# Mask products behind the first mixer's scores, x read and normed first, expert items with two more tiles split ahead of the rows, and an end cut into halves and tiles

## The reference

```
for l in range(DEPTH):                       # first block, DEPTH = 2
    x = x + 0.5 * swiglu(rms_norm(x, ffn1_norm[l]), ffn1_w_in[l], ffn1_w_out[l])
    x = x + hybrid_mixer(rms_norm(x, mix_norm[l]), ...)
    x = x + 0.5 * swiglu(rms_norm(x, ffn2_norm[l]), ...)
```

## Time and profile before

| | us |
|---|---|
| median of 3 runs | 3257.64 (3256.85 to 3260.03) |
| the profiled execution | 3253.87 |
| its span in the trace | 3252.1 |
| PE busy | 3055.1 (94%) |
| DVE busy | 2228.5 (69%) |
| ACT busy | 1767.4 (54%) |
| HBM read | 680.10 MB, 210 GB/s over the span |

### The profile page before, as it was taken

The page is one execution under the profiler, slowest core; times in us unless marked ns, Lnnn a source line. Parts: engine busy times, 40 slices in busy tenths (PEclk is TensorE's granted clock), DMA queues, the critical chain, the costliest instruction groups (busy, mean ns, idle before and its releaser), DMA issues.

```text
span 3252.1 us, 51295 instructions
## 1 busy us (share of the span) xinstructions
PE 3055.1 (94%) x18945; PEld 2671.6 (82%) x18945; DVE 2228.5 (69%) x3150; ACT 1767.4 (54%) x2462; POOL 23.1 (1%) x46
## 2 busy tenths in 40 slices
PE   6999899899989999989999999889989999999996
PEld 5988788799878978888979988787968888888885
DVE  4665665566656666557566676566568998888985
ACT  4345443444544446456444453355467787777874
POOL 0000000000000000000000000000000000000000
PEclk9998999999989999999999999999989999999998
DMA  6863364786425855364578665434459999999995
GB/s 199 270 188 104 104 190 143 256 266 187 150 72 175 252 156 162 104 166 122 162 226 270 190 189 158 137 102 134 117 213 328 363 341 337 340 330 357 342 337 205
DMA packets 662298, 686.63 MB, mean 211 GB/s; under 512 B 22132, under 2 KB 517636, under 8 KB 660804
## 3 DMA queue, kind: packets, MB, share of 16 engines
q1 hardware_dynamic: 658512, 665.22, 63.9%
q0 software_dynamic: 3264, 18.55, 1.6%
q10 hardware_dynamic: 308, 0.09, 0.0%
HBM read 680.10 MB, written 3.67 MB: 210 GB/s over the span
## 4 chain that ended last, share of the span: by engine, by line
PE 82%; DVE 9%; ACT 4%; issue 3%; DMA 1%; DVEq 1%; SPq 0%; ACTq 0%; POOL 0%
PE W L622 30%; PE ACC L622 18%; PE W L705 15%; PE W L706 7%; PE W L615 4%; PE ACC L615 4%; DVE wlo L1626 2%; ACT whi L1211 1%; PE ACC L1015 1%; DVE TT L1652 1%; DVE R L1645 1%; DVE HB L1648 1%; PE ACC L1024 1%; DVE wlo L2047 1%; PE W L1033 1%
## 5 line engine op out<-in xcount | busy, mean ns | idle before, releaser
L1626 DVE TENSOR_TENSOR wlo<-raw,whi 128x1024 fp32r<-128x1024 f32 (+3 forms) x684 | 769.1, 1144 | 487.6 <-ACT whi L1211 485.9
L705 PE MATMUL W<-HB,whi 128*128 128x512 f32 x2112 | 764.2, 404 | 25.7 <-DVE HB L1648 15.7
L1211 ACT ACTIVATE whi<-raw 128x1024 fp32r<-128x1024 f32 (+3 forms) x684 | 658.2, 984 | 66.4 <-DMA raw<-in_ffn_w_in 35.5
L2047 DVE TENSOR_TENSOR wlo<-raw,whi 128x1024 fp32r<-128x1024 f32 x528 | 616.6, 1222 | 85.7 <-ACT whi L1497 79.8
L706 PE MATMUL W<-HB,wlo 128*128 128x256 f32 x2112 | 597.6, 283 | 0.0
L1497 ACT ACTIVATE whi<-raw 128x1024 fp32r<-128x1024 f32 x528 | 544.4, 1059 | 87.0 <-PE W L622 41.1
L622 PE MATMUL W<-HB,whi 128*128 128x256 f32 x2640 | 499.8, 292 | 22.4 <-DVE HB L1648 16.4
L705 PEld LDWEIGHTS W<-HB,whi 128*128 128x128 f32 x2112 | 401.1, 190 | 134.5 <-issue 21.7
L622 PE MATMUL W<-whi,HB 128*128 128x512 f32 (+1 forms) x1664 | 480.6, 374 | 16.5 <-DVE wlo L2047 15.3
L622 PEld LDWEIGHTS W<-HB,whi 128*128 128x128 f32 x2640 | 422.8, 197 | 33.6 <-issue 20.7
L706 PEld LDWEIGHTS W<-HB,wlo 128*128 128x128 f32 x2112 | 404.5, 192 | 0.0
(11 more groups left out here) (385 smaller groups left out, 4023.9 us busy)
## 6 DMA issues: line engine op xcount, KB each, us to landing
raw<-in_moe_w_gate SPq DMA_DIRECT2D x183, 512.0 KB, 5.1
raw<-in_moe_w_up SPq DMA_DIRECT2D x180, 512.0 KB, 5.4
raw<-in_ffn_w_in SPq DMA_DIRECT2D x176, 512.0 KB, 4.1
raw<-in_moe_w_down SPq DMA_DIRECT2D x176, 512.0 KB, 5.4
raw<-in_w_in SPq DMA_DIRECT2D x105, 512.0 KB, 4.1
raw<-in_ffn_w_out SPq DMA_DIRECT2D x88, 512.0 KB, 3.5
scratch<-in_w_mod SPq DMA_DIRECT2D x54, 512.0 KB, 6.9
raw<-in_mix_w_in SPq DMA_DIRECT2D x48, 512.0 KB, 3.7
```

What stands on the lines that cost most here:

```text
L705: mm(o, wh[:, w], HB[:, k, :], start=k == 0, stop=False, skip_group_check=True)
L1211: A_(whi[:, g % SPLIT, 0:LONG[g]], raw[:, g % RAW, 0:LONG[g]], ACT.Copy).then_inc(weight_high, 1)
L1626: V.tensor_tensor(wlo[:, g % RAW, 0:LONG[g]], raw[:, g % RAW, 0:LONG[g]], whi[:, g % SPLIT, 0:LONG[g]].bitcast(F32), ALU.subtract).then_in ...
L2047: V.tensor_tensor(wlo[:, g % RAW, :], raw[:, g % RAW, :], whi[:, g % SPLIT, :].bitcast(F32), ALU.subtract).then_inc(weight_split, 1)
```

## The change

It has four parts.

1. **First mixer.** In `scores` the products of four heads stand back to back and the eight mask products behind them; the second product of a head no longer starts its bank anew. `ret_scores`, `ret_values` and `values` are reordered so that two heads on different halves of the rows or columns alternate. On PE, `sums(0)` moves behind `column(14)`, `rotated` behind `rows(17)`, `sums(1)` behind `column(19)`. `sums(1)` waits for `rot_taken` (the rotation has read ACC) instead of `rot_done`, and `ret_scores` waits for `rot_done`. On ACT the exponential leaves `take` and becomes `invert`, one step later for the first four heads; `soften(0)` and both `weigh` move one step later. On DVE `rotate_all` moves from step 17 to 18.
2. **Start.** SP reads x in two halves first, then 8 vectors, then weights. ACT reads the identity. POOL reads the other 28 vectors, the context and the tables. PE waits for the identity and x alone, ACT squares straight out of PSUM, DVE copies x. Only two units are split ahead of the norm instead of five. The remaining vectors are transposed behind the first `up` unit of the first feed-forward (`first_step(0)`), the context in four pieces behind the units of f = 2 to 5, each copied by ACT one step later. The first modulation reads come at unit 30 instead of 24 and wait for the context's copy; PE waits for the tables only behind this feed-forward.
3. **Expert items.** ACT and DVE split two units (`upto(AHEAD + 2)`, `AHEAD` = 5) before `split_rows`; before, ACT split none and DVE one.
4. **End.** The last rows are weighed, rounded and subtracted in halves; the eight scattered tiles go to eight places, so that no tile waits for a buffer; add, square, sum, scale and transpose run tile by tile, and the output leaves in four DMAs from SP. ACT waits for the unused weight reads later.

```diff
 def scores(i):
-    for b in range(4):
-        h = 4 * i + b
-        q, k = QK1[side(h), h // 2, :], QK1[side(h), 4 + h // 2, :]
-        f32(ACC4[:, b, 0:256], k[:, 0:128], q, True, False)
-        mm(ACC4[:, b, 0:128], identR[:, :], negR[:, :], start=False, stop=True, skip_group_check=True)
-        f32(ACC4[:, b, 256:384], k[:, 128:256], q[:, 128:256], True, False)
-        last = mm(ACC4[:, b, 256:384], identR[:, :], negR[:, :], start=False, stop=True,
-                  skip_group_check=True)
+    for b, q, k in heads:
+        f32(ACC4[:, b, 0:256], k[:, 0:128], q, True, False)
+    for b, q, k in heads:
+        f32(ACC4[:, b, 256:384], k[:, 128:256], q[:, 128:256], False, False)
+    for b in range(4):
+        for c in (0, 256):
+            last = mm(ACC4[:, b, c:c + 128], identR[:, :], negR[:, :], start=False, stop=True,
+                      skip_group_check=True)
...
 def sums(i):
     if i == 1:
-        pe.wait_ge(rot_done, l + 1)
+        pe.wait_ge(rot_taken, l + 1)
...
 column(13)
+column(14)
 sums(0)
-column(14)
 column(15)
 rows(16, 4, 256, 0)
+rows(17, 4, 256, 4)
 rotated()
-rows(17, 4, 256, 4)
 column(18)
+column(19)
 sums(1)
-column(19)
...
 # DVE, step n of mix1
-if n == 17:
+if n == 18:
     rotate_all()
...
 # PE, behind unit "up" f of the first feed-forward
+def first_step(f):
+    if f == 0:
+        pe.wait_ge(vectors_in, 16 * N_VECTORS)
+        for t, n in ((1, 94), (2, 96), (3, 106), (4, 72)):
+            last = nc.tensor.transpose(o[:, t * 128 - 128:t * 128 - 128 + n], rows[0:n, t, :], ident[0:n, 0:n])
+        last.then_inc(params_turned, 1)
+    if 2 <= f < 6:
+        pe.wait_ge(params_taken, 1)
+        if f > 2:
+            pe.wait_ge(c_copied, f - 2)
+        for k in (2 * f - 4, 2 * f - 3):
+            for a in range(2):
...
 # POOL
+for dst, src in vectors[FIRST_V:]:
+    pool.dma_start(dst, src).then_inc(vectors_in, 16)
...
 # DVE, before the first feed-forward
+dve.wait_ge(gains_turned, 1)
 for l in range(2):
-    norm(X, ..., told=l == 1, ahead=start["ffn1", l] + AHEAD)
+    norm(X, ..., told=True, ahead=start["ffn1", l] + (AHEAD if l else 2))
...
 # ACT and DVE, item
-upto(SPLIT)                # DVE only
+upto(AHEAD + 2)
 split_rows()
...
 # DVE, end
-weigh_rows()
-split_rows()
-add_tiles(0).then_inc(dve_to_pe, 1)
-add_tiles(1)
+for c in range(2):
+    V.tensor_scalar(Y[:, c * 512:(c + 1) * 512], YP[:, c * 512:(c + 1) * 512], now[:, 4:5], None, ALU.mult
+                    ).then_inc(rows_weighed, 1)
...
+for d in range(KT):
+    dve.wait_ge(scattered, d // 4 + 1)
...
```

More of the change, by code:

```diff
@@ L488, in program @@
         assert at == 72
-        N_CONST, N_VECTORS = len(CONSTS) + 1, 3 + len(vectors)
-        HALF_V = len(vectors) // 2
+        FIRST_V = 8
+        N_CONST, N_VECTORS = len(CONSTS) + 1, 1 + len(vectors) - FIRST_V
         @block.sync
@@ L566, in _ @@
                     load(MOE + FFU + n, units[n], i)
+            for half in range(2):
+                for a in range(2):
+                    sp.wait_ge(out_copied, 2 * half + a + 1)
+                    cols2 = slice(half * 512, half * 512 + 512)
+                    sp.dma_start(out[0, a * 128:(a + 1) * 128, cols2], S[:, a * 1024 + half * 512:a * 1024 + half * 512 + 512]
+                                 ).then_inc(stored, 16)
+            sp.wait_ge(stored, 64)
         @block.gpsimd
@@ L602, in _ @@
                     pool.dma_start(S[:, 2816:5376], kept[l]).then_inc(kept_in, 16)
-            for a in range(2):
-                pool.wait_ge(act_to_pool, heard.next("act_to_pool"))
-                pool.dma_start(out[0, a * 128:(a + 1) * 128, :], S[:, a * 1024:(a + 1) * 1024]).then_inc(stored, 16)
-            pool.wait_ge(stored, 32)
         @block.tensor
@@ L708, in ffn @@
                     last.then_inc(weight_used, 1)
+                    if name == ("ffn1", 0) and kind == "up":
+                        first_step(f)
                     if name in FILTERS:
@@ L786, in ret_scores @@
                     pe.wait_ge(cum_taken, 2 * l + 2)
-                    for h in range(4):
-                        q, k = QKR[side(h), h // 2, :], QKR[side(h), 2 + h // 2, :]
+                    pe.wait_ge(rot_done, l + 1)
+                    heads = [(h, QKR[side(h), h // 2, :], QKR[side(h), 2 + h // 2, :]) for h in range(4)]
+                    for h, q, k in heads:
                         f32(ACC4[:, h, 0:256], k[:, 0:128], q)
+                    for h, q, k in heads:
                         last = f32(ACC4[:, h, 256:384], k[:, 128:256], q[:, 128:256])
@@ L1269, in ffn, with first_step @@
                 upto(p + N + AHEAD - 1)
+            def first_step(f):
+                if f == 2:
+                    act.wait_ge(params_taken, 1)
+                    for i in range(2):
+                        A_(CS[:, :, i], PV[:, 3, 90 + 8 * i:98 + 8 * i], ACT.Silu)
+                if 3 <= f < 7:
+                    act.wait_ge(c_turned, f - 2)
+                    A_(C[:, 2 * f - 6:2 * f - 4, :], W[:, 3, :].rearrange("p (k t) -> p k t", k=2), ACT.Copy).then_inc(c_copied, 1)
             def mix1(l):
@@ L1527, in item @@
                 upto(FFU + AHEAD)
-            for dst, src in vectors[HALF_V:]:
-                act.dma_start(dst, src).then_inc(vectors_in, 16)
-            act.wait_ge(pe_to_act, heard.next("pe_to_act"))
+            act.dma_start(ident[:, :], A["k_ident"]).then_inc(ident_in, 16)
             for b in range(4):
-                A_(X[:, 2 * b:2 * b + 2, :], ACC[:, 2 * b:2 * b + 2, :], ACT.Copy)
-            act.wait_ge(dve_to_act, heard.next("dve_to_act"))
-            for i in range(2):
-                A_(CS[:, :, i], PV[:, 3, 90 + 8 * i:98 + 8 * i], ACT.Silu)
-            act.wait_ge(pe_to_act, heard.next("pe_to_act"))
-            for b in range(4):
-                A_(C[:, 2 * b:2 * b + 2, :], W[:, b, :].rearrange("p (k t) -> p k t", k=2), ACT.Copy)
-            tell("act_to_pe")
-            tell("act_done")
-            act.wait_ge(act_done, heard.next("act_done"))
+                act.wait_ge(x_turned, b + 1)
+                A_(TT[:, 2 * b:2 * b + 2, :], ACC[:, 2 * b:2 * b + 2, :], ACT.Square).then_inc(x_squared, 1)
             for l in range(2):
-                norm(X, dst=Hhi, after="tiles" if l else "one", ahead=start["ffn1", l] + AHEAD)
+                norm(X, dst=Hhi, after="tiles" if l else "squared", ahead=start["ffn1", l] + (AHEAD if l else 2))
                 if l == 1:
```

190 lines of the change are left out of this document (123 added, 67 removed).

## The result

| | us |
|---|---|
| before, median of 4 runs | 3257.24 (3253.96 to 3260.03) |
| after, median of 4 runs | 3148.10 (3146.69 to 3150.52) |
| after / before | 0.9666, 95% interval 0.9649 to 0.9683 |
| the profiled executions, before and after | 3253.87 and 3147.45 |
| their spans | 3252.1 and 3145.6 |

The change takes 109 us off the median and 106.5 off the span. I had forecast 3173 and a range of 3154 to 3200. The direction, the places and nearly every mechanism were right.

A forecast was written before the change was run, and what follows sets the result against it. PE was taken to bound the kernel, busy 94% of the span, with four places idle or slow. Start 13, mixers 45, pairs 1.5, items 12.5 and end 12 make 84 us less: 3173 us, range 3154 to 3200.

The forecast's parts named there:

- Scores: First mixer: the two scores fall from 7.02 and 9.29 us to 2.9 each, giving back 10.5 us a layer.
- masks at 0.3 each: Mixer scores, bound from the other side: each mask keeps 0.3 us, making 4.1 us a call.
- Clock: Mixer: low-clock excesses of 2.3 (four columns), 1.4 (column 13) and 1.7 (`sums(1)`), 5.4 us a layer, go if PE stays dense.
- Gaps: Mixer: PE's gaps fall from 13.1 us a layer to 0.3, 0.3, 4.2 (before `sums(1)`) and 1.5.
- DVE is the late one: Mixer behind `logits(0)`: DVE needs 2.9 us a step, just PE's 2.88 a unit, plus five long operations.
- Layer 1: Second layer's mixer: the same stretch taken as 78.74 us, to become 22.7 us shorter.
- Pairs: Alternated pairs in `ret_values` and `values`: 0.25 us in each four heads, 1.5 us in all, nothing as lower bound.
- Start: Program start: first product at 22.2, 20.4 us earlier; 4.6 (transposes) and 2.5 (catching up, waits) given back; net 13, between 4 and 18.
- rival 4: Start: POOL's 29 vector DMAs land one behind the other, PE stands from 31 to 158, 3300 us; chance 0.02.
- Items: Expert items: PE's waits for split weights, 15.3 us, shrink to 0.3 at unit 7 per item; gain 12.5, between 0 and 15.3.
- End: Program end: work by halves and tiles, sums at 5.6 us, output finished at 3240; gain 12 us, between 8 and 15.
- Rivals 1 to 3: Mixer gaps stay 13.1 a layer, 3187 (0.14); masks dear and clock low, 3197 (0.09); items gain nothing, 3185 (0.11).

The follow-up runs named there:

- the new order alone: The kernel before with only the order of products and masks in the scores as after; median 3229.12 us.
- head by head: The kernel after with each head's two 64-row products followed by its two masks, 8 changes of rows a call; median 3163.85 us.

## Why the prediction was right or wrong

**What bounds the kernel** was read rightly: the four places with idle or slow PE are where all but some 4 us of the gain lie. The miss is in the sizes. The steps that failed are, largest first, the mixer's gaps (6.3 a layer for a measured 3.55) with layer 1's window (78.74 for 82.18), what the start gives back (7.1 for 3.4), and the durations at the end (12 us less for 16). One by one:

**Scores.** Right in the mechanism and near in size: 2.45 for my 2.9. The bound of masks at 0.3 each falls; they cost 0.11. The price per change was put at 0.28 at most; at clock 1.00 a head of before takes 1.55 (271.50 to 273.05 in its trace), of after 0.61, which is 0.27 for each of 14 changes, and head by head it is 0.40, over that bound.

**Clock.** Right for scores and columns: it is 1.00 through them, and the new order alone brings it back. Wrong for `sums(1)`. Its 1.7 us of excess were to go, with 0.6 given back, and they stayed: behind its wait it takes 5.22 for the 5.27 of before, in after as follows.

```profile
298.98:304.20 5.22, 5.22 (x25) 4.76 (x26) 5.22 (x9) 0.52 (x1) 0.00 (x0) 0.68 0.01 2
```

That the whole of PE's time still fits, 15.1 less in layer 0 (65.50 to 50.41) for my 15.9 less 0.6, is luck: the two calls took 0.9 less than I had, and that covers the 1.1 of `sums(1)`.

**Gaps.** This is the first mis-sized term. The step "DVE is the late one" gave 6.3 us of gaps a layer (0.3, 0.3, 4.2 and 1.5); there are 3.55. The wait before `sums(1)` is 3.17, the one before the retention's scores does not exist, and ACT's evacuation keeps up with the columns. The walk charged DVE 2.9 us for a split and four taps; back to back they take 2.72 in after (292.63 to 295.35). So DVE has read the rotation 43.3 us after the first scores, for my 44.6, and `logits(1)` ends at 50.9, for my 52.5 and before PE is there at 51.5. What the walk did get right is where the one large wait stands, and on whom; the second one, of 1.5, did not come. The terms of the stretch, 49.6, 6.3 and 0.6, also make 56.5 and not the 56 that I wrote.

**Layer 1.** "Layer 1 has the same stretch in 78.74" was false. I ended the window at 947 by the length of layer 0 and did not look for the retention's scores, which start at 950.44. The stretch is 82.18 because the clock was 0.81 in it. The error is 3.4 us, and the row itself had a hint: 374 matmuls where layer 0 has 381.

**Pairs.** 1.5 predicted, 0.16 a layer measured in the one place that shows them alone. What else is in the 4.3 of that row are the two waits of 0.77 and the 1.5 that comes and goes, once in each layer; with the pairs these make 5, of which 0.7 is lost elsewhere.

**Start.** x landed at 6.55 for 7, the norm's sums took 4.7 for 5.4, the first product came at 20.85 for 22.2. The step that failed is what is given back: 7.1 predicted, 3.4 measured. Its 2.5 for catching up is shown to be nothing, beyond 0.7 of waits for ACT. Its 4.6 for the transposes was a slow duration carried into a dense stretch, where four take 0.38 at clock 1.00. These are the windows of that row and of 16 transposes at the end of before.

```profile
18.15:21.83 3.68, 3.68 (x18) 3.68 (x19) 0.00 (x0) 0.00 (x0) 0.00 (x0) 1.00 0.79 223
3240.07:3243.70 3.63, 3.63 (x16) 3.27 (x16) 0.00 (x0) 1.16 (x3) 0.16 (x1) 0.50 0.00 0
```

Both have 0.23 a transpose, the second at clock 0.50. The first reads 1.00 all the same, so at the program's start the clock column would not have warned me; the duration beside a row at a known clock would have.

POOL's vectors were there before PE asked: no wait stands before the transposes at 29.10, so rival 4 did not occur. POOL issued them from 1.25 on, at 0.50 to 0.54 each behind the first. The lock of which the Trainium skill speaks (SBUF — State Buffer, Who interferes with whom) cost nothing that the trace shows.

**Items.** The mechanism was right, unit 7 waits 0.3 at the most. I charged 0.3 to all eight and rounded down; it is 0.19 on average, and the waits shrink by 13.8 (15.3 to 1.5). The items together become 14.9 shorter, so 1.1 of it is busy time that I had at nothing.

**End.** 12 predicted, 16 measured. The sums take 3.81 for my 5.6, which had been read at a lower clock, 0.66; in after the clock is 0.95. From the start of the last DMA issue, at 3142.99, to the end it is 2.6 where I had 5.

**The range.** Each term erred in the same direction, by 22.5 us together (84 to 106.5). The other 3 us of the miss are not in the terms: I put the median 3.8 above the profiled execution, as before, and in after it lies 0.7 above. Twice the reason for a short term is the same, a duration from a slow row carried into a stretch that is dense after the change. Of the terms' own bounds the mixer's (58) and the items' (15.3) held, the start passed its 18 by 0.4 and the end its 15 by 1.0. These bounds together lie 24 us past the sum, and the range reached 19, as if errors in four terms would cancel. It also doesn't follow from what I wrote: halving the distances gives 12 us on the good side and 25 on the other, 3161 to 3198 and not 3158 to 3189. Rivals 1 to 3 did not occur.

**Left open.** Why one change costs 0.27 in the old order and 0.40 head by head is not settled, nor what part of it belongs to the change of type. 0.9 us of the first feed-forward and the 1.5 us that come and go have no cause shown.

## What to carry to other kernels

Group TensorE's products by their number of rows: here 14 changes less a call gave 3.8 us in the call itself at clock 1.00 (four heads of 1.55 against 2.45), and with it the clock came back in stretches that had no change in them. When a duration is carried from one place to another, look at the granted clock of the row first, and at the program's start at the durations too. Where a change makes a stretch dense and the clock rises in it, what stands there gets faster, and estimates from slow rows come out wrong: a gain too small (the sums at the end), or a cost too large (the transposes). And end a window at an instruction that was looked up, not at a length that fitted elsewhere.

## What the runs showed of the hardware

- Changes between 64-row float32 and 128-row float32r products cost 0.27 to 0.40 us each at clock 1.00. A float32r product of 128 columns behind its like costs 0.11.
- The clock fell in stretches where PE was busy in every slice (9.29 us of 9.29 at 0.59), and stayed at 1.00 in the same places once the changes were gone. Behind gaps of about 3 us it was low in some cases and not in others: 0.68 in after's `sums(1)` behind 3.17, and 1.00 in before's `sums(0)` (311.94 to 315.50) behind 3.25.
- Transposes of 128x128 in float32 take 0.23 us at clock 0.50 (end of before) and at the program's start, and about 0.09 inside a dense stretch at 1.00.
- Right behind the start, from 20.85 to 29.10 us of after, the DMA engines moved this (last column, GB/s), nearly twice the 210 of the earlier trace rows:

```profile
20.85:29.10 8.25, 8.25 (x32) 6.34 (x33) 7.48 (x16) 6.85 (x10) 2.20 (x4) 0.70 1.05 390
```
